# The old state of a chunked scan is added on VectorE, on the way out of PSUM, and no longer by an identity product on TensorE

## The chip, the cores and the metric

The kernel runs on one core of a Trainium2 chip. The metric is the device time of one execution in microseconds (us). A run is quoted as the median of several executions, and one further execution was recorded by the hardware profiler. The engines are named as in the profile: PE is TensorE's matrix multiplication, PEld its weight loads, DVE is VectorE, ACT is ScalarE, POOL is GpSimd and SP is SyncE.

## The reference, cut to what matters

One encoder layer is applied to 1024 and to 256 tokens (1280 in all). One of its two mixing branches is a scan in two directions over the tokens, with a 64x64 state for each of eight heads:

```python
def step(S, inp):
    r_t, w_t, k_t, v_t, a_t, b_t = inp
    sa = jnp.einsum('zdhij,zdhj->zdhi', S, a_t)
    S = S * w_t[..., None, :] + sa[..., :, None] * b_t[..., None, :] + v_t[..., :, None] * k_t[..., None, :]
    y = jnp.einsum('zdhij,zdhj->zdhi', S, r_t)
    return S, y
```

Around the scan stand a neighbourhood attention, the projections that feed both branches, the merging of the branches, an output projection and a feed-forward part.

## The kernel before, in words

The kernel is a sequence of stages, and the change lies in one of them, `scan_mixer`. There the scan is done in chunks of C = 64 tokens. The heads are taken in pairs: one tile of 128 partitions holds two heads, 64 partitions each, and CT = 4 such channel tiles (ct) follow each other. The tokens of a tile are cut into NB = 5 blocks (i) of 256 tokens, and each block into GR = 4 chunks (g). A step q is one block of one channel tile, so there are 20 steps and 80 chunks. In every chunk both directions are worked on together: u = 0 is the forward scan, u = 1 the backward scan, side by side along the free dimension, so that a state tile `S` has the shape 128 x 2 x 64, which the trace writes as 128x128.

Each step has two phases. In the first ("levels"), the four chunks go together through five levels of small products, which invert a triangular matrix; their states don't take part. In the second, which this text calls the state phase, the four chunks go one after the other, because each needs the state that the one before it left. For chunk g, PE has this order of work, written out by hand in the queue:

- `state_in` waits for the token tile and for the state (`s_ready`), then multiplies `GM` by `TK` (L567) and adds the product of `AR` and the old state `S` (L571). ACT copies the result to `PT` (L852).
- `gram_products` of the next step, chunk g - 1 (L500), 128 columns wide; for g = 0 there are none.
- `solved` (L581) waits for `PT`; ACT copies the result to `UT` (L854).
- `by_token` of the next step, chunk g - 1 (L513, L516, L519); for g = 0 there are none.
- `state_out` waits for `UT` (`u_ready`), and then accumulates in PSUM, for each direction: the old state times the identity (L592), `TK` by `TK` (L595), and `TK` by `UT` (L598). The last product releases `s_ps`.
- `outputs` (L607, L611, L614) makes the chunk's outputs, from the old state in L611.

After g = 3 come the gram products and the `by_token` products of the fourth chunk of the next step (L500, L513 to L519), then the next step's `turn` (L531). Every line above is two products for each direction (one for each head); the trace records two instructions for each product, so a row "x4" of one of these lines is one direction.

DVE has in the same phase, for chunk g: for g > 0 the mask of the next step's chunk g - 1 (L887, L890, L894; a wait for its own result stands between each two of them), then a wait for `s_ps` and the multiplication of the new state by the chunk's decays `edge` (L980), which releases `s_ready`, then a wait for `y_ps` and the output of the chunk (L986 or L992).

At the start of a sequence there is no old state. `fresh(i, u, g)` says so: it holds at g = 0 for i = 0 in both directions, for i = 4 in the forward one, and for i = 1 in the backward one. There L571, L592 and L611 leave that direction out.

POOL prepares the arrays of the next step (`AR`, `edge`), and DVE and ACT do side work of other channel tiles between the levels. The last step has no next one, so its chunks have neither gram nor `by_token` products between them.

Of the kernel before, what the change touches and what calls it, by code (L numbers as in the profile page):

```python
# [6 lines left out]
ALU = mybir.AluOpType  # L7
AX = mybir.AxisListType

P = 128  # L10
# [16 lines left out]
C = 64  # L27
# [3 lines left out]
NB = T // BT  # L31
NB_P = TP // BT
GR = BT // C
# [273 lines left out]
def scan_mixer(nc, lora, params, cn_scan, ones, mean, sT):  # L307

    with ExitStack() as ctx:
        sb = lambda n, s: ctx.enter_context(nc.sbuf_tensor(n, s, F32))  # L310
        sems = []

        def sem(n):
            sems.append(nc.alloc_semaphore("sc_" + n))
            return sems[-1]
# [6 lines left out]
        eye, neg_eye = cs[:, CS_I:CS_I + C], cs[:, CS_I + C:CS_I + 2 * C]  # L322
# [14 lines left out]
        AI, Q1, PT, UT = ([sb(f"sc_{n}{g}", [P, 2, C]) for g in range(GR)]  # L337
                          for n in ("ai", "q", "pt", "ut"))
        S = [sb(f"sc_s{n}", [P, 2, C]) for n in range(2)]

        ps = ctx.enter_context(nc.psum_tensor("sc_ps", [P, 8, 512], F32))
        units = lambda b, lo, n: ps[:, b, lo:lo + 2 * n].rearrange("p (u t) -> p u t", u=2)
# [4 lines left out]
        p_out, u_out, s_out = (units(STATE_BANK, n * 2 * C, C) for n in range(3))  # L347
# [22 lines left out]
        heads = (slice(0, HD), slice(HD, P))  # L370
        col = lambda ct, n: params[:, PM_RK + ct * NPC + n:PM_RK + ct * NPC + n + 1]

        def chunk(u, g):

            at = (g if u == 0 else GR - 1 - g) * C
            return slice(at, at + C)
# [15 lines left out]
        def fresh(i, u, g):  # L392

            return g == 0 and (i == 0 or i == (NB_P if u == 0 else NB - NB_P))
# [77 lines left out]
        def _(pe):  # L472
# [86 lines left out]
            def state_in(q, g):  # L559
# [4 lines left out]
                for u in range(2):  # L564
# [4 lines left out]
                    if not new:  # L569
                        for rows in heads:  # L570
                            last = nc.tensor.matmul(p_out[rows, u, :], AR[q % 2][rows, 0, u, chunk(u, g)],  # L571
                                                    S[n % 2][rows, u, :], start=False, stop=True)
                last.then_inc(p_ps, 1)
# [9 lines left out]
                last.then_inc(u_ps, 1)  # L583

            def state_out(q, g):
                i, n = q % NB, q * GR + g
                pe.wait_ge(u_ready, n + 1)
                for u in range(2):
                    new = fresh(i, u, g)
                    if not new:  # L590
                        for rows in heads:
                            nc.tensor.matmul(s_out[rows, u, :], eye[rows, :], S[n % 2][rows, u, :],  # L592
                                             start=True, stop=False)
                    for rows in heads:
                        nc.tensor.matmul(s_out[rows, u, :], TK[g][rows, u, 1, :], TK[g][rows, u, 2, :],  # L595
                                         start=new, stop=False)
                    for rows in heads:
                        last = nc.tensor.matmul(s_out[rows, u, :], TK[g][rows, u, 0, :], UT[g][rows, u, :],  # L598
                                                start=False, stop=True)
                last.then_inc(s_ps, 1)  # L600

            def outputs(q, g):
                i, n = q % NB, q * GR + g
                for u in range(2):
# [4 lines left out]
                    if not new:  # L609
                        for rows in heads:  # L610
                            nc.tensor.matmul(q_out[g][rows, u, :], S[n % 2][rows, u, :],  # L611
                                             AR[q % 2][rows, 1, u, chunk(u, g)], start=False, stop=False)
# [86 lines left out]
            for q in range(STEPS):  # L699
                ct, i = divmod(q, NB)  # L700
# [171 lines left out]
        def _(dve):  # L872
            def cumulate(q, n):
                if n < 2:
                    way = slice(None) if n == 0 else slice(None, None, -1)
                    dve.wait_ge(sg_ready, q + 1)
                    nc.vector.tensor_tensor_scan(cum[:, n, way], reset, lw[:, n, way], 0.0,
                                                 ALU.mult, ALU.add).then_inc(cum_own, 1)
                else:
                    dve.wait_ge(cum_own, 2 * q + 2)  # L880
                    nc.vector.tensor_tensor(lw[:, :, :], cum[:, :, :], lw[:, :, :], ALU.subtract
                                            ).then_inc(cum_ready, 1)

            def mask(q, g):
                n = q * GR + g
                dve.wait_ge(gram, n + 1)
                nc.vector.tensor_tensor(GM[g][:, :, :, :].rearrange("p u n t -> p (u n t)"),  # L887
                                        ps[:, GRAM_BANK, :], gmask, ALU.mult).then_inc(masked, 1)
                dve.wait_ge(masked, n + 1)
                nc.vector.tensor_tensor(AI[g][:, :, :], GM[g][:, :, 0, :],  # L890
                                        eye.unsqueeze(1).to_broadcast([P, 2, C]), ALU.add
                                        ).then_inc(ai_ready, 1)
                dve.wait_ge(ai_ready, n + 1)
                nc.vector.tensor_tensor(XY[g][:, 1, :, :], AI[g][:, :, :], first, ALU.mult  # L894
                                        ).then_inc(y1_ready, 1)
# [29 lines left out]
            def side(ct, i, l, g):  # L925
                c, slot = ct - 1, l * GR + g
                bank = TOK_BANK if l == 1 else GRAM_BANK
                if i == 0 and ct > 0 and l < NG and g == 3:
                    centre(c, l, bank)
                if i == 2 and ct > 0 and l < NG and g == 3:  # L930
                    bonus_out(c, l, bank)
                if i == 2 and ct + 1 < CT and slot < T // P:
                    dve.wait_ge(nrm_ready, (ct + 2) * NG)
                    last = nc.vector.reciprocal(nrm[:, tenth(slot)], nrm[:, tenth(slot)])
                    if slot == T // P - 1:
                        last.then_inc(rn_ready, 1)
                if i == 2 and ct + 1 < CT and T // P <= slot < T // P + NB:
                    unit_k(ct + 1, slot - T // P)
                if i == 1 and ct > 0 and slot % 2 == 1 and slot // 2 < NB:
                    bonus_in(c, slot // 2)  # L940
                if i == 3 and ct > 0 and slot < T // P:
                    dve.wait_ge(std_ready, ct * NG)
                    last = nc.vector.reciprocal(std[:, tenth(slot)], std[:, tenth(slot)])
                    if slot == T // P - 1:
                        last.then_inc(rs_ready, 1)
                if i == 4 and ct > 0 and 1 <= l <= NG and g == 3:
                    gated(c, l - 1, TOK_BANK if l == 2 else GRAM_BANK)
# [13 lines left out]
            for q in range(STEPS):  # L961
                ct, i = divmod(q, NB)
                more = q + 1 < STEPS
                for l in range(LEVELS):
                    for g in range(GR):
                        nth = (q * LEVELS + l) * GR + g + 1
                        dve.wait_ge(q_ps, nth)
                        nc.vector.tensor_tensor(Q1[g][:, :, :].rearrange("p u t -> p (u t)"),  # L968
                                                ps[:, g, 0:2 * C], joins[:, l, :], ALU.mult
                                                ).then_inc(q_ready, 1)  # L970
                        if more and l == 1 and g < 3:
                            cumulate(q + 1, g)
                        side(ct, i, l, g)
                for g in range(GR):
                    n = q * GR + g
                    if more and g:
                        mask(q + 1, g - 1)
                    at = i * GR + g
                    dve.wait_ge(s_ps, n + 1)
                    nc.vector.tensor_tensor(S[(n + 1) % 2][:, :, :], s_out,  # L980
                                            edge[q % 2][:, g, :].unsqueeze(2).to_broadcast([P, 2, C]),
                                            ALU.mult).then_inc(s_ready, 1)
                    dve.wait_ge(y_ps, n + 1)
                    chunks = y[ct % 2][:, :].rearrange("p (n t) -> p n t", t=C)
                    if 2 * at < NC:
                        nc.vector.tensor_copy(chunks[:, at:NC - at:NC - 1 - 2 * at, :], q_out[g]  # L986
                                              ).then_inc(y_ready, 1)
                    else:
                        far = NC - 1 - at
                        pair = chunks[:, at:(far - 1 if far else None):far - at, :]  # L990
                        dve.wait_ge(y_ready, ct * NB * GR + far + 1)
                        nc.vector.tensor_tensor(pair, pair, q_out[g], ALU.add).then_inc(y_ready, 1)  # L992
                if more:
                    mask(q + 1, GR - 1)
# [970 lines left out]
```

## Time and profile before

| | |
|---|---|
| median of 3 runs | 3081.03 us (3078.32 to 3084.27) |
| the profiled execution: its time | 3081.26 us |
| the profiled execution: its span, first to last instruction | 3079.6 us |
| mean granted PE clock over the span | 0.945 |
| PE busy | 2688.3 us (87%) |
| DVE busy | 1342.3 us (44%) |
| ACT busy, POOL busy | 723.3 us (23%), 827.6 us (27%) |

The profile is of one execution. Busy shares are averages over stages with different limits, so what a change in one stage is worth has to be read from that stage. A granted clock of 1.00 is the upper of PE's two levels (2.4 GHz), 0.5 the lower (1.2 GHz). Ends of matmuls are modelled; the starts of the weight loads are the sharper marks of PE's pace.

### The profile page before, as it was taken

What the parts mean: (1) busy time and instruction counts of PE and PEld (TensorE: products, weight loads), DVE (VectorE), ACT (ScalarE), POOL (GpSimd) and SP (SyncE); (2) the same over time, 40 slices, a digit from 0 to 9 for tenths busy, and PEclk for the clock granted to TensorE, in tenths of its full rate; (3) what the DMA queues carried; (4) which work ended last, traced back from release to release, by engine and by line L of the source; (5) the groups of instructions that cost most, each with busy time, mean ns of one, the idle gap of its engine ahead of it and who ended that gap; (6) DMA issues with size and microseconds to landing.
All of it is one profiled execution on the core that took longest, in us unless ns stands there. A gap on an engine that the chain in (4) does not pass through costs nothing. (4 is left out here: it accounts for less than half of the span.)

```text
span 3079.6 us, 67727 instructions
## 1 busy us (share of the span) xinstructions
PE 2688.3 (87%) x28944; PEld 2213.5 (72%) x28944; DVE 1342.3 (44%) x2284; ACT 723.3 (23%) x1604; POOL 827.6 (27%) x576
## 2 busy tenths in 40 slices
PE   3976997997995888888888859778899999999997
PEld 3864446886884788687778845457688888888886
DVE  5002783551113343554444432366545454454555
ACT  3101551110002444444344421113110110110102
POOL 1321112332331222232132310153432332323324
PEclk6987998998997999999999989989899999999999
DMA  3013012102221000000000014333111110101113
GB/s 99 27 45 58 16 30 76 41 20 74 80 75 46 3 3 3 3 3 3 3 3 3 3 63 145 131 113 109 63 47 34 41 41 27 48 34 34 41 48 123
DMA packets 60139, 143.05 MB, mean 46 GB/s; under 512 B 12064, under 2 KB 31136, under 8 KB 59424
## 3 DMA queue, kind: packets, MB, share of 16 engines
q1 hardware_dynamic: 46128, 114.36, 11.3%
q10 hardware_dynamic: 10256, 12.49, 1.3%
q0 software_dynamic: 3552, 13.11, 1.1%
q8 instruction: 175, 2.87, 0.4%
q14 instruction: 28, 0.23, 0.0%
HBM read 108.48 MB, written 31.46 MB: 45 GB/s over the span
## 5 line engine op out<-in xcount | busy, mean ns | idle before, releaser
L1822 DVE TENSOR_TENSOR f<-f,ff_pd 128x512 f32<-128x512 f32 x320 | 214.3, 684 | 153.1 <-PE ff_pd L94 153.0
L1808 DVE TENSOR_TENSOR ff_sq<-ff_rl 128x512 f32<-128x512 f32 (+1 forms) x96 | 102.9, 1072 | 296.4 <-ACT ff_rl L1769 296.4
L1769 ACT ACTIVATE ff_rl<-ff_pu 128x512 f32<-128x512 f32 (+1 forms) x96 | 50.6, 527 | 759.9 <-PE ff_pu L94 759.9
L552 PE MATMUL sc_ps<-sc_q,sc_xy 64*64 64x64 f32 x2560 | 170.1, 229 | 35.7 <-DVE sc_q L968 34.6
L555 PE MATMUL sc_ps<-sc_xy,sc_q 64*64 64x64 f32 x3200 | 188.3, 225 | 0.1
L968 DVE TENSOR_TENSOR sc_q<-sc_ps,sc_cs 128x128 f32<-128x128 f32 x400 | 101.9, 279 | 169.6 <-PE sc_ps L543 168.9
L543 PEld LDWEIGHTS sc_ps<-sc_xy,sc_ai 64*64 64x64 f32 x3200 | 114.0, 140 | 74.7 <-ACT sc_xy L820 57.7
L552 PEld LDWEIGHTS sc_ps<-sc_q,sc_xy 64*64 64x64 f32 x2560 | 134.7, 142 | 45.7 <-DVE sc_q L968 44.9
L820 ACT ACTIVATE sc_xy<-sc_ps 128x256 f32<-128x256 f32 x320 | 122.3, 384 | 190.5 <-PE sc_ps L555 184.7
L543 PE MATMUL sc_ps<-sc_xy,sc_ai 64*64 64x64 f32 x3200 | 136.9, 229 | 33.7 <-ACT sc_xy L820 32.2
L555 PEld LDWEIGHTS sc_ps<-sc_xy,sc_q 64*64 64x64 f32 x3200 | 156.2, 141 | 0.2 <-DVE sc_q L968 0.2
L94 PE MATMUL ff_pu<-h2h,ff_wu0h 128*128 128x512 f32 (+1 forms) x384 | 136.9, 356 | 15.0 <-POOL ff_wu0l L1717 15.0
L418 POOL TENSOR_SCALAR sc_fac<-sc_icl,params,sc_k1a 128x512 f32<-128x512 f32 x20 | 17.6, 880 | 485.7 <-ACT sc_icl L759 485.7
L94 PE MATMUL ff_pu<-h2l,ff_wu0h 128*128 128x512 f32 (+1 forms) x384 | 136.6, 356 | 0.0
L94 PE MATMUL ff_pu<-h2h,ff_wu0l 128*128 128x512 f32 (+1 forms) x384 | 136.5, 356 | 0.0
L94 PE MATMUL ff_pu<-h2l,ff_wu1h 128*128 128x512 f32 (+1 forms) x384 | 136.0, 354 | 0.0
L94 PE MATMUL ff_pu<-h2h,ff_wu1h 128*128 128x512 f32 (+1 forms) x384 | 135.9, 354 | 0.0
L94 PE MATMUL ff_pu<-h2h,ff_wu1l 128*128 128x512 f32 (+1 forms) x384 | 135.8, 354 | 0.0
L94 PE MATMUL ff_pd<-ff_wd0h,ff_gh 128*128 128x512 f32 x320 | 126.6, 395 | 10.1 <-DVE f L1822 10.0
L1714 POOL TENSOR_TENSOR ff_wd0h<-ff_wr,params 128x1024 fp32r<-128x1024 f32 x16 | 30.3, 1896 | 356.5 <-PE ff_pd L94 356.4
L94 PE MATMUL ff_pd<-ff_wd0l,ff_gh 128*128 128x512 f32 x320 | 124.7, 390 | 0.0
L94 PE MATMUL ff_pd<-ff_wd1h,ff_gh 128*128 128x512 f32 x320 | 124.7, 390 | 0.0
(274 smaller groups left out, 7458.2 us busy)
## 6 DMA issues: line engine op xcount, KB each, us to landing
ff_wr<-in_w_up SPq DMA_DIRECT2D x32, 512.0 KB, 3.3
ff_wr<-in_w_down SPq DMA_DIRECT2D x32, 512.0 KB, 3.3
g_dram<-gp_g ACTq DMA_DIRECT2D x16, 640.0 KB, 3.0
mb_gate<-g_dram SPq DMA_DIRECT2D x8, 1280.0 KB, 9.1
gp_w<-in_w_in SPq DMA_DIRECT2D x16, 512.0 KB, 3.5
sp_w<-in_w_in SPq DMA_DIRECT2D x15, 512.0 KB, 3.5
n_x<-in_x SPq DMA_DIRECT2D x10, 512.0 KB, 3.6
m_dram<-mb_mo POOLq DMA_DIRECT2D x8, 640.0 KB, 8.6
```

The lines of the kernel that those rows point to most:

```text
L94: mm = nc.tensor.matmul(out, stationary[a], moving[b], start=first and n == 0, stop=last and n == len(pairs) - 1)
L418: nc.gpsimd.tensor_scalar(fac[:, :, :], icl[:, :, :], col(ct, K_A), k1a[:, ct:ct + 1], ALU.mult, ALU.add).then_inc(prep_own, 1)
L543: last = nc.tensor.matmul(q_out[g][rows, u, :], AI[g][rows, u, :], XY[g][rows, 0, u, :], start=True, stop=True)
L552: nc.tensor.matmul(x_out[g][rows, u, :], XY[g][rows, 1, u, :], Q1[g][rows, u, :], start=True, stop=True)
L555: last = nc.tensor.matmul(y_out[g][rows, u, :], Q1[g][rows, u, :], XY[g][rows, 1, u, :], start=True, stop=True)
L820: nc.scalar.activation(XY[g][:, :, :, :].rearrange("p n u t -> p (n u t)"), ps[:, g, 2 * C:6 * C], ACT.Copy).then_inc(xy_ready, 1)
L968: nc.vector.tensor_tensor(Q1[g][:, :, :].rearrange("p u t -> p (u t)"), ps[:, g, 0:2 * C], joins[:, l, :], ALU.mult).then_inc(q_ready, 1)
L1714: nc.gpsimd.tensor_tensor(to[0], wr[m % 2][:, :], zero_like(wr[m % 2][:, :], zero), ALU.add).then_inc(high_done, 1)
L1769: nc.scalar.activation(rl[u % 2][:, 0:tn], pu[b][:, 0:tn], ACT.Relu).then_inc(relu, 1)
L1808: nc.vector.tensor_tensor(sq[u % 2][:, 0:tn], rl[u % 2][:, 0:tn], rl[u % 2][:, 0:tn], ALU.mult).then_inc(squared, 1)
L1822: nc.vector.tensor_tensor(at, at, pd[d % 4][:, :], ALU.add).then_inc(added, 1)
```

## The change

The identity products (L592) are taken out of `state_out`. DVE instead reads the accumulated PSUM result, adds the old state `S[n % 2]` to it, and writes the sum to a new SBUF tile `grown`; then it waits for its own result on a new semaphore and multiplies `grown` by `edge` into the next state, where it formerly multiplied straight from PSUM. In chunks with a fresh direction the first pass is done in two instructions of 128x64, one for each direction: a copy where the direction is fresh, an addition where it isn't. In all other chunks it is one 128x128 addition.

```diff
         S = [sb(f"sc_s{n}", [P, 2, C]) for n in range(2)]
+        grown, grown_ready = sb("sc_grown", [P, 2, C]), sem("grown")
...
             def state_out(q, g):
-                i, n = q % NB, q * GR + g
+                n = q * GR + g
                 pe.wait_ge(u_ready, n + 1)
                 for u in range(2):
-                    new = fresh(i, u, g)
-                    if not new:
-                        for rows in heads:
-                            nc.tensor.matmul(s_out[rows, u, :], eye[rows, :], S[n % 2][rows, u, :],
-                                             start=True, stop=False)
                     for rows in heads:
                         nc.tensor.matmul(s_out[rows, u, :], TK[g][rows, u, 1, :], TK[g][rows, u, 2, :],
-                                         start=new, stop=False)
+                                         start=True, stop=False)
...
                     dve.wait_ge(s_ps, n + 1)
-                    nc.vector.tensor_tensor(S[(n + 1) % 2][:, :, :], s_out,
+                    if any(fresh(i, u, g) for u in range(2)):
+                        for u in range(2):
+                            if fresh(i, u, g):
+                                nc.vector.tensor_copy(grown[:, u, :], s_out[:, u, :]).then_inc(grown_ready, 1)
+                            else:
+                                nc.vector.tensor_tensor(grown[:, u, :], s_out[:, u, :], S[n % 2][:, u, :],
+                                                        ALU.add).then_inc(grown_ready, 1)
+                    else:
+                        nc.vector.tensor_tensor(grown[:, :, :], s_out, S[n % 2][:, :, :], ALU.add
+                                                ).then_inc(grown_ready, 2)
+                    dve.wait_ge(grown_ready, 2 * n + 2)
+                    nc.vector.tensor_tensor(S[(n + 1) % 2][:, :, :], grown[:, :, :],
                                             edge[q % 2][:, g, :].unsqueeze(2).to_broadcast([P, 2, C]),
                                             ALU.mult).then_inc(s_ready, 1)
```

## Rows read from the trace of the kernel before

**Rows 1.** Busy time by stretch: the scan, then single chunks, from one L980 to the next.

```profile
core 0: us, PE busy (x) PEld busy (x) DVE busy (x) ACT busy (x) POOL busy (x), PEclk, DMA share, GB/s
985.00:1812.00 827.00, 726.64 (x18558) 651.93 (x18555) 376.54 (x979) 362.00 (x922) 209.93 (x196) 0.97 0.01 3
1213.62:1218.85 5.23, 5.21 (x111) 5.10 (x108) 1.86 (x6) 1.05 (x3) 0.00 (x0) 0.67 0.01 3
1218.85:1222.52 3.67, 3.67 (x120) 3.67 (x116) 1.85 (x5) 1.04 (x3) 0.00 (x0) 1.00 0.00 0
1797.83:1801.18 3.35, 2.52 (x75) 2.27 (x72) 0.57 (x2) 0.56 (x2) 0.00 (x0) 1.00 0.01 2
```

**Rows 2.** One line: the DVE product that makes the new state, and its waits.

```profile
L980 DVE TENSOR_TENSOR sc_s<-sc_ps,sc_edge x80: 290/292/293, 1013.5 to 1807.9; 128x128 f32<-128x128 f32 x80
its engine sat idle before it (us, times) until:
  PE sc_ps L598: 98.3, 80
who waited for it (us, times):
```

**Rows 3.** Timeline, step 0, chunk 2: start, duration, engine, line, operation (idle before it).

```profile
1019.83 0.23 PEld L592 LDWEIGHTS sc_ps<-sc_s,sc_cs 64*64 64x64 f32 x4
1019.92 0.29 DVE L890 TENSOR_TENSOR sc_ai<-sc_gm,sc_cs 128x128 f32<-128x128 f32 x1
1020.18 0.23 PEld L592 LDWEIGHTS sc_ps<-sc_s,sc_cs 64*64 64x64 f32 x4
1020.24 0.29 DVE L894 TENSOR_TENSOR sc_xy<-sc_ai,sc_cs 128x128 f32<-128x128 f32 x1
1020.42 0.23 PEld L598 LDWEIGHTS sc_ps<-sc_ut,sc_tk 64*64 64x64 f32 x4
1020.53 0.23 PEld L607 LDWEIGHTS sc_ps<-sc_gm,sc_tk 64*64 64x64 f32 x4
1020.82 0.29 DVE L980 TENSOR_TENSOR sc_s<-sc_ps,sc_edge 128x128 f32<-128x128 f32 x1 [0.29 <-PE sc_ps L598]
1021.23 0.23 PEld L567 LDWEIGHTS sc_ps<-sc_tk,sc_gm 64*64 64x64 f32 x4
1021.52 0.29 DVE L986 COPY sc_y<-sc_ps 128x128 f32<-128x128 f32 x1 [0.41 <-PE sc_ps L614]
```

**Rows 4.** Timeline, step 0, chunk 0, where both directions are fresh.

```profile
1013.49 0.29 DVE L980 TENSOR_TENSOR sc_s<-sc_ps,sc_edge 128x128 f32<-128x128 f32 x1 [2.84 <-PE sc_ps L598]
1013.57 0.20 PEld L614 LDWEIGHTS sc_ps<-sc_gm,sc_ut 64*64 64x64 f32 x4
1013.89 0.22 PEld L567 LDWEIGHTS sc_ps<-sc_tk,sc_gm 64*64 64x64 f32 x4
```

**Rows 5.** Timeline, step 8, chunk 0, with POOL at work.

```profile
1347.25 2.92 POOL L450 TENSOR_TENSOR sc_y<-sc_y,sc_std 128x1280 f32<-128x1280 f32 x1
...
1349.22 0.29 DVE L980 TENSOR_TENSOR sc_s<-sc_ps,sc_edge 128x128 f32<-128x128 f32 x1 [3.31 <-PE sc_ps L598]
...
1349.65 0.20 PEld L567 LDWEIGHTS sc_ps<-sc_tk,sc_gm 64*64 64x64 f32 x4
```

**Rows 6.** Timeline, step 19, chunk 2: the last hand-over of a state inside a step.

```profile
1804.54 0.29 DVE L980 TENSOR_TENSOR sc_s<-sc_ps,sc_edge 128x128 f32<-128x128 f32 x1 [2.38 <-PE sc_ps L598]
...
1804.97 0.20 PEld L567 LDWEIGHTS sc_ps<-sc_tk,sc_gm 64*64 64x64 f32 x4
```

**Rows 7.** Timeline, end of step 0's state phase.

```profile
1024.49 0.29 DVE L980 TENSOR_TENSOR sc_s<-sc_ps,sc_edge 128x128 f32<-128x128 f32 x1 [0.29 <-PE sc_ps L598]
...
1024.96 1.07 PE L500 MATMUL sc_ps<-sc_ar 64*64 64x128 f32 x16
1025.19 0.29 DVE L986 COPY sc_y<-sc_ps 128x128 f32<-128x128 f32 x1 [0.41 <-PE sc_ps L614]
```

**Rows 8.** Groups by line and shape: the removed products, and DVE operations near the new ones.

```profile
L592 PE MATMUL sc_ps<-sc_s,sc_cs 64*64 64x64 f32 x576 | 43.7, 221 | 5.5 <-ACT sc_ut L854 5.5
L894 DVE TENSOR_TENSOR sc_xy<-sc_ai,sc_cs 128x128 f32<-128x128 f32 x79 | 23.0, 292 | 2.7
L992 DVE TENSOR_TENSOR sc_y<-sc_y,sc_ps 128x128 f32<-128x128 f32 x40 | 11.5, 288 | 15.9 <-PE sc_ps L614 15.9
L1286 DVE TENSOR_SCALAR sT<-at_o 128x64 f32 x80 | 17.5, 219 | 7.3 <-PE at_o L1209 7.3
```

**Rows 9.** Timeline: four DVE products in a row with no wait on each other.

```profile
1344.92 0.99 DVE L968 TENSOR_TENSOR sc_q<-sc_ps,sc_cs 128x128 f32<-128x128 f32 x4 [1.81 <-PE sc_ps L543]
```

## The prediction

> **What bounds the kernel now.** I read the busy time by stretch first. The scan takes 827 us of the 3079.6 us span, PE is busy for 726.64 us of it, DVE for 376.54 us, and the granted clock averages 0.97; a single chunk of the state phase, from one L980 to the next, takes 3.67 us in which PE is busy for all 3.67 us and DVE for 1.85 us [rows 1]. The reader is to see that this phase has no gap on PE. Then I read the one line that makes the new state: L980 always waits for PE's L598, 80 times, and nobody is listed as having waited for L980 [rows 2]. Taken alone that says that DVE's product is free. So I read the timeline of one chunk, to see how nearly it is late. The new state is written from 1020.82 to 1021.11, and the load that needs it (L567 of the next chunk, behind `s_ready`) starts at 1021.23, which is 0.12 us later [rows 3]. In the first chunk of all, which has shorter outputs, PE has run out of work (its last L614 load starts at 1013.57, and one takes 0.12 us of PE's pace) and does wait for the state: it ends at 1013.78 and the load starts at 1013.89, 0.11 us later [rows 4]. So 0.11 us is the hand-over from DVE to this load, and the usual chunk has 0.01 us to spare. In step 8 the two are 1349.51 and 1349.65, 0.03 us to spare [rows 5]. There are 60 places where one chunk's state is taken by the next chunk of its step; from the first to the last (1804.83 to 1804.97) I read 0.11 to 0.15 us [rows 4, 6]. PE is the bound, with a chain through DVE of practically the same length beside it.
>
> **What is removed.** L592 has 576 records, so 144 directions: 160 of 80 chunks, less the 16 fresh ones [rows 8]. In a dense chunk six such rows (L592, L595, L598 for each direction) take from 1019.83 to 1020.53, so one direction of one line costs 0.70 / 6 = 0.117 us and an ordinary chunk loses 0.233 us [rows 3]. They stand behind the wait for `u_ready` and ahead of the last L598, so they lie both on PE's queue and on the chain to the new state: all of it counts in either case. If nothing came back, that would be 144 x 0.117 = 16.8 us.
>
> **What is added.** The first pass reads PSUM and an SBUF tile, as L992 does (288 ns); the second reads two SBUF operands, as L894 does (292 ns), and L980 itself took 292 ns [rows 2, 8]. None is cheaper by its source. Between them is DVE's wait for its own result, as between L890 and L894, whose starts are 0.32 us apart [rows 3]; I take 0.325 us, since the neighbouring pairs read 0.32 or 0.33. So the state comes 0.325 us later after the last L598 than it did. Bounds: without the wait, four products took 0.99 us, (0.99 - 0.29) / 3 = 0.23 us apart [rows 9], and that is the lower end; the upper end is a wait that costs as much as the hand-over from DVE to PE, 0.29 + 0.11 = 0.40 us [rows 4].
>
> VectorE's own table speaks for a cheaper second pass: the Trainium skill (VectorE: DVE Perf Modes, section on the TRN2 errata) gives 58 cycles plus one for each element from SBUF and 120 from PSUM, which at 0.96 GHz would be an estimate of 194 ns against 258 ns. This trace has 292 and 292 ns for the two kinds [rows 2, 8], so it disagrees; the same section's other formula, (N+151)/0.96, gives 291 ns and fits. By the table the sum below would come out about 4 us lower.
>
> With a fresh direction the first pass is two 128x64 instructions with no wait between them. A 128x64 read of PSUM takes 219 ns [rows 8]. Two in a row start 0.23 us apart at 128x128, and 64 elements fewer take 0.07 us less (292 - 219 = 73 ns), so 0.16 us [rows 8, 9]. The product starts 0.16 + 0.22 + 0.03 = 0.41 us after the first, rounded up to 0.43 us for a possible hold between a copy and an addition; bounds 0.33 us and 0.50 us (two whole 219 ns and the gaps).
>
> **What hides it.** The next `state_in` can't move up, since PE's queue is in order and its wait stands before L567 too. Only the outputs lie between, 0.70 us [rows 3], and they are used up but for the spare 0.01 to 0.03 us. PE then idles. The chain behind that point doesn't change its length: a stalled `state_in` at 1013.89 and a dense one at 1021.23 are each followed by the same sequence. After g = 3 no `state_in` follows but the gram products, 1024.96, of which neither the wait nor the data hang on the state [rows 7]: there the 0.233 us is kept whole. Queued behind the new wait on DVE are the chunk's output and the next mask. The output starts at 1021.52, held by PE [rows 3]; counted from the last L598 load (1020.42) that is 1.10 us, and the second pass is over 0.40 + 0.325 + 0.29 = 1.02 us after it, so nothing moves. In front of the add stands the mask: L894 is over at 1020.53 and the state's PE work would now end at 1020.82 - 0.233 = 1020.59, so the add still waits for PE, with 0.06 us left [rows 3]. If that were gone, each 0.01 us would cost at most 0.7 us over 68 chunks. POOL writes during L980 in step 8 and L980 takes its usual 0.29 us [rows 5], so I put no contention into the sum.
>
> **The sum.** By kinds of chunk:
> - 48 ordinary chunks followed by another in their step: +0.325 - 0.02 (spare) - 0.233 = +0.072 us each, +3.5 us.
> - 8 first chunks with one fresh direction (i = 1 and 4): +0.43 - 0.01 - 0.117 = +0.30 us, +2.4 us.
> - 4 first chunks with both fresh (nothing removed, PE already waits): +0.43 us, +1.7 us.
> - 20 last chunks of a step: -0.233 us, -4.7 us. The last step has no gram products, but the queue goes on there with outputs that cover the state too.
>
> Together +2.9 us: 16.8 us are taken from PE and about 19.7 us come back as waits for the state. On the profiled execution's own 3081.26 us that makes 3084.2 us; the median of the runs is 3081.03 us, 0.2 us lower, so I say 3084.0 us, or +0.1%. About 0.2%, 6 us, is what a measurement of this kernel can tell from no change. A chunk would go from 3.67 to about 3.74 us.
>
> **Rivals.**
> 1. The added pass is hidden. The list of those who waited for L980 is empty [rows 2]. If the state had had time to spare, only the removal would count: 3081 - 16.8 = 3064 us, faster. It decides from the point where the spare time exceeds 0.325 - 0.233 = 0.09 us in the ordinary chunks; the rows show 0.01 to 0.03 us [rows 3, 5]. Chance 5%.
> 2. PE's clock. The granted clock falls to its lower level in short stretches, and one such stretch in the state phase cost 5.23 - 3.67 = 1.56 us [rows 1]. New idle time of 0.3 us in 60 chunks may bring more. One more in every fourth step: 5 x 1.56 = 7.8 us on top, 3092 us, slower; two more are enough to cross 6 us. Against it: in the last step PE is busy for only 2.52 of 3.35 us and the clock stayed at 1.00 [rows 1], a looser chunk than the new ones (3.4 of 3.74 us). Chance 17%. The same shifts could take such stretches away, which is 3% for a gain over 6 us.
> 3. DVE's own wait costs 0.11 us and not 0.03: +0.08 x 60 = 4.8 us, 3089 us. The gap between L890 and L894 speaks against it [rows 3]. Chance 7%.
> 4. The product from SBUF is shorter, by 0.065 us x 60 = 3.9 us: 3080 us, no measurable change. It is the table's rule named above; L894's 292 ns speaks against it [rows 8]. Chance 8%.
>
> **The numbers.** The forecast has 60%, and its own range is 3080 to 3088 us (the spread of the three runs, 6 us, and the bounds on the fresh chunks, +-1 us). Within 0.2% are the forecast and rival 4, and a little of both neighbours: 70%. Slower by more are rivals 2 and 3: 22%. Faster by more are rival 1 and a luckier clock: 8%. For 8 times in 10 the range needs the lower bound of the spacing (0.23 us: -0.095 x 60 = -5.7 us, 3078 us) and rival 3 (3089 us), and a part of rival 2: 3077 to 3090 us.
>
> **What would show it.** In the profile after: L592's records gone (PE 576 fewer), L500 to L614 unchanged in number; 68 additions 128x128 of some 288 ns, 24 of the 128x64 kind, and 80 products from SBUF of 292 ns; PE waiting for that product at about 60 places, 0.3 us each in ordinary chunks, so some 20 us in all; chunks of 3.74 us inside a step; the way from the last state of a step to the next `turn` unchanged. The prediction is wrong if PE's wait for the state is under 0.2 us, if the add waits for the mask and not for PE, or if the low-clock stretches in the scan change in number.

## The result, and the profile after

The changed kernel takes 3088.4 us (median of 8 runs, 3086.44 to 3090.73) against 3080.56 us for the kernel before (8 runs, 3076.52 to 3084.31). The ratio is 1.0026, with a 95% interval from 1.0015 to 1.0037, so it is 8 us slower (4.6 to 11.4 us). The forecast was 3084.0 us, or 3 us more than before. The sign and the range for 8 times in 10 (3077 to 3090 us) held. The size was too small by 5 us: 3088.4 us lies just outside the forecast's own range (3080 to 3088 us), and 0.26% just outside the likeliest class ("within 0.2%").

The page of the changed kernel, its first lines, and the busy time of the scan and of one chunk (columns as in [rows 1]):

```profile
span 3084.8 us, 66735 instructions
PE 2679.2 (87%) x28368; PEld 2198.5 (71%) x28368; DVE 1367.4 (44%) x2376; ACT 722.6 (23%) x1604; POOL 825.0 (27%) x576
```

```profile
985.00:1816.00 831.00, 715.89 (x17984) 636.23 (x17981) 400.01 (x1068) 360.97 (x921) 210.07 (x196) 0.97 0.01 3
1018.04:1021.86 3.82, 3.64 (x111) 3.53 (x109) 2.14 (x6) 1.04 (x3) 0.00 (x0) 1.00 0.01 4
```

PE has 28368 matmul records and had 28944, exactly 576 fewer. The granted clock in the scan is 0.97 as before. A chunk takes 3.82 us where it took 3.67 [rows 1]. The other chunks grew alike: the median over the 60 places where a chunk hands its state to the next of its step is 3.83 us (3.825), against 3.67 us (3.673) before.

The timeline of step 0, chunk 2, the one of [rows 3] (rows left out here are marked by "..." or are of PE's matmuls):

```profile
1020.71 0.23 PEld L591 LDWEIGHTS sc_ps<-sc_tk 64*64 64x64 f32 x4
...
1021.06 0.23 PEld L594 LDWEIGHTS sc_ps<-sc_ut,sc_tk 64*64 64x64 f32 x4
1021.12 0.29 DVE L890 TENSOR_TENSOR sc_xy<-sc_ai,sc_cs 128x128 f32<-128x128 f32 x1
...
1021.54 0.29 DVE L984 TENSOR_TENSOR sc_grown<-sc_ps,sc_s 128x128 f32<-128x128 f32 x1
...
1021.76 0.23 PEld L610 LDWEIGHTS sc_ps<-sc_gm,sc_ut 64*64 64x64 f32 x4
1021.86 0.29 DVE L987 TENSOR_TENSOR sc_s<-sc_grown,sc_edge 128x128 f32<-128x128 f32 x1
1022.17 0.29 DVE L993 COPY sc_y<-sc_ps 128x128 f32<-128x128 f32 x1
1022.27 0.22 PEld L568 LDWEIGHTS sc_ps<-sc_tk,sc_gm 64*64 64x64 f32 x4 [0.28 <-issue]
```

Count from the last weight load of the state's product (L598 before, L594 now). Before: the DVE product starts 0.40 us after it and the next chunk's load 0.81 us after it [rows 3]. Now the addition starts at 0.48, the product at 0.80, it ends at 1.09, and the load of the next chunk starts at 1.21 us. PE's last output load is at 1021.76, it is done with it some 0.12 us later, and then it stands still. The 0.40 us that the load has lost are more than the 0.23 us by which the chunk's own work has shrunk.

The list of waits gives the sum. PE's weight loads at L568, the next chunk's first product, had 2.3 us of idle time in 2 places before; now it is

```profile
PEld sc_ps L568 <- issue: 22.2, 61, 1.1
```

For the weight loads the releaser is given as "issue" and not as DVE, though the timeline shows the load starting 0.12 us after the product's end in each of the 60 places. The matmuls behind these loads are put down to the DVE product:

```profile
PE sc_ps L568 <- DVE sc_s L987: 13.5, 58, 0.8
```

So the record can name DVE, and the list of [rows 2] was empty because PE still had work until just before the load. Such a list holds the longer waits, and not who nearly had to wait. In the version with the raise by 1 below, whose gap is 0.07 us shorter, it names the product at 14 places only, though the load follows the product by 0.12 us at all 60.

The two DVE lines of the change; the second has a maximum of 929 ns:

```profile
L984 DVE TENSOR_TENSOR sc_grown<-sc_ps,sc_s x68: 290/291/292, 1017.7 to 1813.2; 128x128 f32<-128x128 f32 x68
L987 DVE TENSOR_TENSOR sc_s<-sc_grown,sc_edge x80: 291/291/929, 1014.2 to 1813.6; 128x128 f32<-128x128 f32 x80
```

There are three such long ones, in steps 8, 13 and 18, always chunk 0. The first of them, with POOL beside it:

```profile
1349.03 2.89 POOL L451 TENSOR_TENSOR sc_y<-sc_y,sc_std 128x1280 f32<-128x1280 f32 x1
1350.83 0.29 DVE L984 TENSOR_TENSOR sc_grown<-sc_ps,sc_s 128x128 f32<-128x128 f32 x1 [3.14 <-PE sc_ps L594]
1351.16 0.92 DVE L987 TENSOR_TENSOR sc_s<-sc_grown,sc_edge 128x128 f32<-128x128 f32 x1
```

This is the place of [rows 5], where L980 took 0.29 us beside the same POOL instruction. Those three chunks take 4.45 or 4.46 us in place of 3.83. In all three L987 ends 0.15 us after POOL's product does. The trace of the kernel before already holds such cases among DVE's side work, with two SBUF tiles as operands. L900 took 479 ns in the median, 1586 ns at the longest, and 1.28 us in this one:

```profile
L900 DVE SCALAR_TENSOR_TENSOR sc_kk<-sT,params,sc_nrm x20: 472/479/1586, 969.2 to 1512.7; 128x256 f32<-128x256 f32 x20
1298.25 1.44 POOL L440 TENSOR_TENSOR sc_ar<-sc_ar,sc_neg 128x512 f32<-128x512 f32 x1
1298.69 1.28 DVE L900 SCALAR_TENSOR_TENSOR sc_kk<-sT,params,sc_nrm 128x256 f32<-128x256 f32 x1
```

### The profile page after: what moved, and what is told of

It is laid out like the page before. It is cut to its first block and busy times, and to the rows that moved or that the text cites. A ratio compares the mean times of both kernels' runs of the same rounds, so it can differ in the third digit from the quotient of the medians.

```text
span 3084.8 us, 66735 instructions
## 1 busy us (share of the span) xinstructions
PE 2679.2 (87%) x28368; PEld 2198.5 (71%) x28368; DVE 1367.4 (44%) x2376; ACT 722.6 (23%) x1604; POOL 825.0 (27%) x576
## 3 DMA queue, kind: packets, MB, share of 16 engines
q1 hardware_dynamic: 46128, 114.36, 11.4%
```

## The experiments

Differences to the kernel before are ratios of the runs times 3080 us, with their 95% interval; the medians are given where a forecast was a time. "Chunk" is the median over the 60 hand-overs, from one state to the next.

**The two halves of the change.** DVE's part alone: the identity product stays, and DVE copies and then multiplies.

```diff
-                    nc.vector.tensor_tensor(S[(n + 1) % 2][:, :, :], s_out,
+                    nc.vector.tensor_copy(grown[:, :, :], s_out).then_inc(grown_ready, 2)
+                    dve.wait_ge(grown_ready, 2 * n + 2)
+                    nc.vector.tensor_tensor(S[(n + 1) % 2][:, :, :], grown[:, :, :],
```

> The kernel before with the DVE part alone: the identity product stays on PE, DVE copies PSUM to the new tile (raising the semaphore by 2), waits and multiplies. Main theory (the state is on the path of every chunk, with no time to spare): a chunk goes from 3.67 to about 4.05 us and the kernel gets 60 x 0.385 = 23 us slower (3104 us). Rival (the added pass is mostly hidden, and the loss of the change came from somewhere else): under 8 us slower. If the addition's late start comes from the raise by 2 the copy starts at 0.47 us too; if it comes from reading the old state as well, at 0.40 us, and the chunk takes 3.98 us (19 us slower).

Measured: 3103.56 us, +22.5 us (18.2 to 26.8), chunk 4.06 us. The rows of step 0, chunk 2:

```profile
1020.93 0.23 PEld L599 LDWEIGHTS sc_ps<-sc_ut,sc_tk 64*64 64x64 f32 x4
1021.41 0.29 DVE L981 COPY sc_grown<-sc_ps 128x128 f32<-128x128 f32 x1 [0.36 <-PE sc_ps L599]
1021.73 0.29 DVE L983 TENSOR_TENSOR sc_s<-sc_grown,sc_edge 128x128 f32<-128x128 f32 x1
...
1022.14 0.22 PEld L568 LDWEIGHTS sc_ps<-sc_tk,sc_gm 64*64 64x64 f32 x4 [0.28 <-issue]
```

The pass is paid in full: 0.39 us a chunk. The copy doesn't read the old state and starts late (0.48 us) all the same, which leaves the raise by 2 under suspicion.

PE's part alone, which leaves the old state out of the new one and so doesn't compute the scan:

```diff
-                    new = fresh(i, u, g)
-                    if not new:
-                        for rows in heads:
-                            nc.tensor.matmul(s_out[rows, u, :], eye[rows, :], S[n % 2][rows, u, :],
-                                             start=True, stop=False)
...
-                                         start=new, stop=False)
+                                         start=True, stop=False)
```

> The kernel before with the PE part alone: the identity products are left out and nothing takes their place, so that the old state is not carried into the new one (that part of the computation is missing). Main theory: 144 directions x 0.117 us = 16.8 us faster (3064 us), a chunk takes 3.44 us. Rival (PE's removed work was hidden too, so that the change only added): no change.

Measured: 3066.29 us, -13.9 us (-17.9 to -9.5), chunk 3.44 us. The chunk is as expected, and the 16.8 us are inside the interval. The halves add up: 22.5 - 13.9 = +8.6 us, against +8 us for the whole change, and in the chunk 0.386 - 0.233 = 0.153 us, against 0.152 us.

**Why the addition starts late.** The raise by 1:

```diff
-                        nc.vector.tensor_tensor(grown[:, :, :], s_out, S[n % 2][:, :, :], ALU.add
-                                                ).then_inc(grown_ready, 2)
-                    dve.wait_ge(grown_ready, 2 * n + 2)
+                        nc.vector.tensor_tensor(grown[:, :, :], s_out, S[n % 2][:, :, :], ALU.add
+                                                ).then_inc(grown_ready, 1)
+                    dve.wait_ge(grown_ready, passes)
```

> The changed kernel, with the 128x128 addition raising its semaphore by 1 and not by 2 (the waits are counted accordingly). In the changed kernel the addition starts 0.47 us after the last weight load of the state's product, where the old multiplication started 0.40 us after it. Theory A1: the raise by 2 delays the start; then it starts at 0.40 us, a chunk takes 3.75 us and not 3.82, and the kernel gains 60 x 0.07 = 4 us (3084 us). Theory A2: reading PSUM and the old state, or the size, delays it; then nothing changes (3088 us, 0.47 us, 3.82 us).

Measured: 3086.25 us, +5.9 us (3.1 to 8.6), chunk 3.76 us. Step 0, chunk 2:

```profile
1021.90 0.23 PEld L594 LDWEIGHTS sc_ps<-sc_ut,sc_tk 64*64 64x64 f32 x4
1021.96 0.29 DVE L890 TENSOR_TENSOR sc_xy<-sc_ai,sc_cs 128x128 f32<-128x128 f32 x1
1022.31 0.29 DVE L986 TENSOR_TENSOR sc_grown<-sc_ps,sc_s 128x128 f32<-128x128 f32 x1
1022.63 0.29 DVE L989 TENSOR_TENSOR sc_s<-sc_grown,sc_edge 128x128 f32<-128x128 f32 x1
...
1023.04 0.22 PEld L568 LDWEIGHTS sc_ps<-sc_tk,sc_gm 64*64 64x64 f32 x4 [0.21 <-issue]
```

The addition starts 0.41 us after the load, and the chunk is 0.07 us shorter. Theory A1 holds in the trace; in the time the two intervals overlap (1.0019, 1.0010 to 1.0028, against 1.0026, 1.0015 to 1.0037), so there it is not shown by itself. The mask in front of the addition is not the cause. In the last step there is none, and the addition of the changed kernel still starts 0.46 us after the load; with the raise by 1 it starts 0.39 us after it there:

```profile
1805.75 0.20 PEld L594 LDWEIGHTS sc_ps<-sc_ut,sc_tk 64*64 64x64 f32 x4
1806.21 0.29 DVE L984 TENSOR_TENSOR sc_grown<-sc_ps,sc_s 128x128 f32<-128x128 f32 x1 [2.71 <-PE sc_ps L594]
```

**POOL and the second pass.** The sum stays in PSUM:

```diff
-                        nc.vector.tensor_tensor(grown[:, :, :], s_out, S[n % 2][:, :, :], ALU.add
+                        nc.vector.tensor_tensor(s_out, s_out, S[n % 2][:, :, :], ALU.add
...
-                    nc.vector.tensor_tensor(S[(n + 1) % 2][:, :, :], grown[:, :, :],
+                    nc.vector.tensor_tensor(S[(n + 1) % 2][:, :, :], s_out,
```

> The changed kernel with the raise by 1, and the sum of product and old state written back into PSUM in place of the new SBUF tile, so that the second pass reads PSUM and one SBUF operand. Theory: the three second passes that took 0.93 us and not 0.29 (step 8, 13 and 18, chunk 0) were held because they read two SBUF operands while POOL ran its product of two SBUF tiles (L450 in the rows of before); with a PSUM operand all 80 take 0.29 us and the kernel gains 3 x 0.64 = 1.9 us against the raise by 1. Rival (POOL's presence slows any DVE pass there): these three stay at 0.9 us. A chunk should stay at 3.76 us if a PSUM write costs what an SBUF write does.

Measured: 3083.44 us, +4.6 us (1.8 to 7.7), chunk 3.76 us. The second pass with the sum in SBUF (the version with the raise by 1), and then with it in PSUM:

```profile
L989 DVE TENSOR_TENSOR sc_s<-sc_grown,sc_edge x80: 291/293/999, 1015.1 to 1815.6; 128x128 f32<-128x128 f32 x80
```

```profile
L989 DVE TENSOR_TENSOR sc_s<-sc_ps,sc_edge x80: 290/291/292, 1015.0 to 1811.6; 128x128 f32<-128x128 f32 x80
```

The long ones are gone, and POOL's product (L451) still runs over all three places; the three chunks take 3.76 us, where they took 4.46 us. So here a DVE product with two SBUF operands is held by POOL's product of two SBUF tiles, and one with a PSUM operand isn't. Each of the five versions with such a product has three held ones (0.70 to 1.02 us), and each of these ends 0.15 us after POOL's product. In the time the 2 us are not shown: the intervals of +4.6 and +5.9 us overlap.

**What PE's gap is.** The wait for the state moved behind products that don't need it, first in the changed kernel (with the raise by 1), then in the kernel before:

```diff
-        p_out, u_out, s_out = (units(STATE_BANK, n * 2 * C, C) for n in range(3))
+        p_out, u_out = (units(STATE_BANK, n * 2 * C, C) for n in range(2))
+        s_out = units(LORA_BANK, 0, C)
...
-                if n:
-                    pe.wait_ge(s_ready, n)
                 for u in range(2):
                     new = fresh(i, u, g)
                     for rows in heads:
                         last = nc.tensor.matmul(p_out[rows, u, :], GM[g][rows, u, 2, :], TK[g][rows, u, 2, :],
                                                 start=True, stop=new)
+                    if n and u == 0:
+                        pe.wait_ge(s_ready, n)
```

> The changed kernel with the raise by 1, and the wait for the new state moved behind the first direction's L567 products, which don't need it (the state's product goes to the bank of the LoRA products, so that DVE's reading and these products are in different banks). Main theory (PE stands still for 0.3 us in every chunk until the state is there): work moved into that gap is free, 0.117 us in 60 places, a chunk goes from 3.76 to 3.65 us and the kernel from 3086 to 3079 us. Rival (the time between the chunks is not a wait but set by PE's own restart): no change against the raise by 1.

> The same move in the kernel before, as the control. There the state has 0.01 to 0.03 us to spare, so PE doesn't wait and there is no gap to fill: a chunk stays at 3.67 us, and the kernel gains nothing that can be measured (under 2 us). If the bank or the order as such were worth something, it would show here.

Measured: the changed kernel with the move 3069.24 us, -8.9 us (-12.3 to -5.9), chunk 3.56 us; the kernel before with it -1.5 us (-4.3 to +1.2), chunk 3.67 us. The control is as expected. The first gained more than it should have: 0.20 us a chunk against the version with the raise by 1, and not 0.117. Its rows of the hand-over:

```profile
1018.91 0.29 DVE L990 TENSOR_TENSOR sc_s<-sc_grown,sc_edge 128x128 f32<-128x128 f32 x1
1019.02 0.20 PEld L567 LDWEIGHTS sc_ps<-sc_tk,sc_gm 64*64 64x64 f32 x4
1019.26 0.20 PEld L573 LDWEIGHTS sc_ps<-sc_s,sc_ar 64*64 64x64 f32 x4
```

The state is there at 1019.20 and its reader starts at 1019.26: the median hand-over is 0.05 us, where it was 0.12 us in every version that waits for the token tile and for the state at the same product. So the hand-over itself was tested, with the wait for the token tile done once ahead of the four chunks and everything else as in the version with the raise by 1, and again in the kernel before:

```diff
-                pe.wait_ge(tok_ready, n + 1)
                 if n:
                     pe.wait_ge(s_ready, n)
...
                 side_clear(ct, i)
+                pe.wait_ge(tok_ready, (q + 1) * GR)
                 for g in range(GR):
```

> The changed kernel with the raise by 1, and PE's wait for the token tile taken out of the front of every chunk and done once ahead of the state phase (it has long been met there), so that the next chunk's first product has the wait for the state alone in front of it. Theory: in the version with the wait for the state behind the first L567 products the hand-over from DVE to PE took 0.05 us and not 0.12, because only one wait stood there; then a chunk goes from 3.76 to 3.69 us and the kernel gains 60 x 0.07 = 4 us against the raise by 1 (3082 us, or 1 to 2 us above before). Rival (the 0.05 us came from the order of the products or the bank): 3.76 us and no change.

> The same in the kernel before, as the control: the state gets 0.07 us more to spare, but PE is dense, so a chunk stays at 3.67 us and the time does not change by more than 1 to 2 us.

Measured: 3082.32 us, +2.8 us (0.0 to 5.5), chunk 3.67 us; the control -0.6 us (-3.4 to +2.2), chunk 3.67 us. Step 0, chunk 2 of the first:

```profile
1020.51 0.29 DVE L986 TENSOR_TENSOR sc_grown<-sc_ps,sc_s 128x128 f32<-128x128 f32 x1
...
1020.84 0.29 DVE L989 TENSOR_TENSOR sc_s<-sc_grown,sc_edge 128x128 f32<-128x128 f32 x1
...
1021.18 0.20 PEld L567 LDWEIGHTS sc_ps<-sc_tk,sc_gm 64*64 64x64 f32 x4 [0.16 <-DVE sc_s L989]
```

The load now starts 0.05 us after the product, and the list of waits names DVE for it. A wait that has long been met still cost 0.06 us (medians of 0.116 and 0.053 us) where it stood in front of the same product as the wait that counts. The chunk is 0.08 us shorter (3.758 to 3.675), 0.02 us more than that accounts for, which stays open; the version with the move has the same 0.02 us (0.117 + 0.063 of its 0.20 us). In the time the gain is not shown by itself, since the intervals of +2.8 and +5.9 us overlap.

**A version that keeps the gain.** First the old state times the decays was made ahead of time, and the new state in two fused instructions:

```diff
+                    for u in range(2):
+                        e = edge[q % 2][:, g, u:u + 1]
...
+                            now = nc.vector.scalar_tensor_tensor(S[(n + 1) % 2][:, u, :], s_out[:, u, :], e,
+                                                                 aged[:, u, :], ALU.mult, ALU.add)
...
+                        nc.vector.tensor_tensor(aged[:, :, :], S[(n + 1) % 2][:, :, :],
+                                                edge[qn % 2][:, gn, :].unsqueeze(2).to_broadcast([P, 2, C]),
+                                                ALU.mult).then_inc(aged_ready, 1)
```

> Identity products left out; DVE multiplies the old state by the decays right after it is made, off the path, and makes the new state with two fused instructions of 128x64 (PSUM times decay plus the aged state), one for each direction. Main theory: what hurts is only what lies between the last product and the state. Two 128x64 instructions take 0.16 + 0.22 = 0.38 us where the one multiplication took 0.29, so the state is 0.09 to 0.12 us later and a chunk takes 3.67 - 0.233 + 0.10 = 3.54 us; the kernel is 16.8 - 60 x 0.10 = 11 us faster than before (3070 us). Rival (any added DVE work in the state phase costs its whole length, 0.29 us more here): 6 to 8 us slower than before.

Measured: 3080.58 us, +0.6 us (-2.2 to +3.4), chunk 3.68 us. Both theories missed: the chunk was to take 3.54 us, or the kernel to be 6 to 8 us slower. Step 0, chunk 2:

```profile
1020.61 0.23 PEld L595 LDWEIGHTS sc_ps<-sc_ut,sc_tk 64*64 64x64 f32 x4
...
1021.09 0.47 DVE L984 SCALAR_TENSOR_TENSOR sc_s<-sc_ps,sc_edge,sc_aged 128x64 f32<-128x64 f32 x2
...
1021.60 0.29 DVE L993 TENSOR_TENSOR sc_aged<-sc_s,sc_edge 128x128 f32<-128x128 f32 x1
1021.68 0.22 PEld L569 LDWEIGHTS sc_ps<-sc_tk,sc_gm 64*64 64x64 f32 x4
```

The pair starts at 0.48 us and not 0.40, though neither of its instructions raises a semaphore by 2. It has two waits in front of it, for `aged` and for the product; whether these are the cause on DVE was not tested. And it takes 0.47 us and not 0.38, since one fused instruction of 128x64 takes 280 ns. The aged product behind it lies off the path: the load still follows the pair by 0.12 us, and in steps 8, 13 and 18, where POOL holds it for 0.73 us, the chunk stays at 3.68 us. Then each direction got its own bank and its own signal, and two of the three mask instructions were moved behind the state:

```diff
+        s_out = [ps[:, LORA_BANK, 0:C], ps[:, STATE_BANK, 4 * C:5 * C]]
...
-                last.then_inc(s_ps, 1)
+                    last.then_inc(s_ps, 1)
...
+                        dve.wait_ge(s_ps, 2 * n + u + 1)
...
-                        mask(q + 1, g - 1)
+                        mask_gram(q + 1, g - 1)
...
+                    if more and g:
+                        mask_first(q + 1, g - 1)
```

> The fused version (old state aged off the path) with what it lacked: each direction's product in a PSUM bank of its own with its own signal, so that the first direction's fused instruction runs while PE makes the second's product, and only the first of the three mask instructions stands in front of them on DVE. In the fused version without this the state was there 0.95 us after the last weight load; here it is one fused instruction of 128x64 after it, 0.48 + 0.22 = 0.70 us, and with the hand-over of 0.12 us that is 0.82 us, just when PE has finished the outputs. Main theory: PE doesn't wait, a chunk takes 3.44 us, and all of the 16.8 us is kept: 3063 us. Rival (the state's own path still sets the chunk): 3.55 us or more and less than 10 us faster than before.

Measured: 3062.94 us, -13.9 us (-17.9 to -9.5), chunk 3.45 us, the same as with PE's part alone. It is faster than both kernels, and unlike PE's part alone it computes the whole scan. The rows, and the busy time of one chunk:

```profile
1019.44 0.23 PEld L596 LDWEIGHTS sc_ps<-sc_ut,sc_tk 64*64 64x64 f32 x4
...
1019.68 0.47 DVE L992 SCALAR_TENSOR_TENSOR sc_s<-sc_ps,sc_edge,sc_aged 128x64 f32<-128x64 f32 x2 [0.54 <-PE sc_ps L596]
...
1020.14 0.23 PEld L612 LDWEIGHTS sc_ps<-sc_gm,sc_ut 64*64 64x64 f32 x4
1020.27 0.22 PEld L570 LDWEIGHTS sc_ps<-sc_tk,sc_gm 64*64 64x64 f32 x4
```

```profile
1016.23:1019.68 3.45, 3.45 (x112) 3.45 (x109) 2.24 (x7) 1.05 (x4) 0.00 (x0) 1.00 0.02 5
```

The pair is over 0.71 us after the last load, the next chunk's load starts at 0.83 us, and PE is busy for all of the 3.45 us. PE and the chain now end together: the last output load (L612) starts at 1020.14 and takes some 0.12 us of PE's pace, and the pair ends at 1020.15, with the usual hand-over of 0.12 us behind it. So this version has nothing to spare either. How much the banks and signals brought, and how much the moved mask instructions, was not run separately.

## Why the prediction was right, and where its size was off

**Two paths of the same length.** This step carried the forecast, and it held. PE's part alone gave 3.44 us a chunk, DVE's part alone 4.06 us, and filling PE's gap helped the changed kernel and not the one before. Rival 1 (the pass is hidden) is out: the empty list of those who waited said nothing of the 0.01 to 0.03 us that were left.

**What is removed.** 576 records and 0.233 us a chunk, as worked out (3.67 to 3.44 us).

**What is added.** The spacing of 0.325 us between the passes was right (0.32 to 0.33 us in the trace), and so was 0.29 us for either pass; the cheaper product of rival 4 isn't there. The Trainium skill (VectorE: DVE Perf Modes, section on the TRN2 errata) has a table that sets a read from SBUF below one from PSUM, and L984 and L987 with 291 ns each don't bear it out. Rival 3 put DVE's wait for its own result at 0.11 us; it is 0.03.

**The step that was mis-sized.** I took the addition to start where the old product had started, 0.40 us after the last load, and spoke of the mask in front of it as the only thing that could delay it. It started at 0.47 to 0.48 us. The diff shows why, and I read past it: it raises its semaphore by 2. That is 0.07 us in the chunks with a whole addition. In 48 of the 60 hand-overs the cost was 0.152 us net (3.673 to 3.825 us) in place of 0.072, or 4 us in all. The terms known (0.325 + 0.07 - 0.02 - 0.233) give 0.142 us of it; the last 0.01 us has no cause shown.

**A term set to nothing.** "I put no contention into the sum" rested on L980 beside POOL [rows 5]. L980 read PSUM; the new product reads two SBUF tiles. Three places at 4.45 - 3.83 = 0.62 us are 1.9 us. The row was read for the instruction that was there, not for the one that would come; L900 in the same trace would have shown the hold.

**Fresh chunks.** 0.43 us was taken; the product starts 0.38 to 0.39 us after the first of the pair, which has a raise by 1 and starts at 0.38 us: the split costs about the same as the whole. That is 0.5 us less than forecast over 12 chunks.

**The last chunks of a step** keep their gain: between the state of step 1's last chunk and of step 2's first 31.21 us passed before and 30.99 us now (from 1067.35 to 1098.34), 0.22 us less. That is one of 19 such stretches. They scatter from 0.2 us more to 1.6 us less, with low-clock stretches in different places, and their median is 0.21 us less.

With the measured terms the sum is 48 x 0.152 + 8 x (0.39 - 0.01 - 0.117) + 4 x 0.39 - 20 x 0.233 + 1.9 = 7.3 + 2.1 + 1.6 - 4.7 + 1.9 = +8.2 us, against the measured +8 us.

**The clock (rival 2)** isn't needed for the result, but two profiles can't be compared without it. The recorded executions differ by only 5.2 us (spans of 3079.6 and 3084.8 us). After the stretch at the lower level that ends at 985 us, the scan has ten such stretches in either trace, partly in other places: 51 us in all before and 44 us after. At half the clock those 7 us are worth 3.4 us at most, and 5.2 + 3.4 = 8.6 us is near the +8 us of the medians again. The mean of 0.97 in both is too coarse to show this.

**What was luck.** The result fell into the class "slower by more than 0.2%", which had its 22% from rivals 2 and 3, and neither of them came about. The range of 3077 to 3090 us held by the room that had been left for them; what used it was the raise by 2, which the prediction had not seen, and POOL, which it had put at nothing.

## What to carry to other kernels

Where PE is dense but a chain through another engine is within hundredths of a microsecond of it, work moved from PE to that chain is paid in full, and what PE saves turns into waiting. Look at the time between the state's end and its reader's start, not only at the list of waits. Ask of the moved work which part needs the late operand: here the old state could be aged ahead of time, and only one short instruction had to stay behind the product. Then look at how the hand-over is written: the amount of the raise, waits that stand together, and the memory that each operand comes from.

## What the runs showed of the hardware

- A DVE instruction that raises a semaphore by 2 was recorded as starting 0.07 us later than the same one with a raise by 1 (0.48 against 0.41 us after the last load), and everything behind it moved with it.
- Two dependent 128x128 DVE passes with a wait on a semaphore between them started 0.32 to 0.33 us apart, with 0.29 us for the first.
- A long-met wait in front of the same product as the wait that counts made the hand-over from DVE to PE 0.12 us in place of 0.05 us, in the median of 60 places.
- A 128x128 DVE product of two SBUF operands took 0.70 to 1.02 us beside POOL's product of two SBUF tiles and ended 0.15 us after it, and took 0.29 us with one operand in PSUM.
- An addition that writes its result back to PSUM took 298 ns, against 291 ns into SBUF.
